# Small products of preparation and readout, one behind each visit of the chain

## The reference

```
zd = z + mu[d] * (shift_seq(z, offset) - z)
r, k, v, lw, la = split(zd)
decay = exp(-exp(-softplus(-(w0[d] + tanh(lw) @ w2[d])) - 0.5))
a = sigmoid(a0[d] + la @ a2[d])
kk = k * k_k;  kk = kk * rsqrt(max(sum_per_head(kk * kk), 1e-24))
k = k * (1 + (a - 1) * k_a)
S = S * decay + (S @ -kk) (kk * a)^T + v k^T;  y = S r     # per token, both directions
bonus = sum_per_head(r * k * r_k) * v
y = (y - mean(y)) * rsqrt(var(y) + eps) * lnx_g + lnx_b + bonus;  y = y * (sigmoid(lg) @ g2)
```

## Time and profile before

| | us |
|---|---|
| median of 3 runs | 3356.26 |
| lowest, highest | 3355.75, 3357.25 |
| profiled execution, its span | 3357.8 |

### The profile page before, as it was taken

How to read it: one execution, slowest core, us unless ns; L and a number is a source line. 1 busy time by engine, 2 the same in 40 slices (tenths; PEclk the granted TensorE clock), 3 DMA queues, 4 the chain that set the end, 5 groups by cost and what they waited for, 6 DMA issues and landing times.

```text
span 3357.8 us, 79208 instructions
## 1 busy us (share of the span) xinstructions
PE 3114.1 (93%) x34382; PEld 2493.0 (74%) x34382; DVE 1500.2 (45%) x2358; ACT 1162.7 (35%) x2403; POOL 831.6 (25%) x518
## 2 busy tenths in 40 slices
PE   7999898999999998999999888989899989989998
PEld 5777676778777786888888666767667667768886
DVE  4455473745444653100144464756565456330033
ACT  4433333423334424211112353434333345342222
POOL 2211111111123132222223221111111243434453
PEclk9999999999999999999999989999999999999999
DMA  5424242434454441111111233413233343522222
GB/s 212 135 97 145 81 142 101 130 121 144 145 166 151 158 169 57 51 63 62 62 50 63 75 101 98 127 63 120 65 122 106 93 140 115 188 69 95 99 88 75
DMA packets 246714, 364.56 MB, mean 109 GB/s; under 512 B 154080, under 2 KB 155376, under 8 KB 245904
## 3 DMA queue, kind: packets, MB, share of 16 engines
q1 hardware_dynamic: 226976, 294.57, 27.6%
q10 hardware_dynamic: 14976, 35.66, 2.7%
q0 software_dynamic: 4464, 29.92, 2.5%
HBM read 290.88 MB, written 69.21 MB: 107 GB/s over the span
## 4 chain that ended last, share of the span: by engine, by line
PE 76%; DVE 6%; issue 5%; ACT 4%; DMA 2%; DVEq 2%; POOLq 2%; PEld 1%; SPq 1%; POOL 0%; PEldq 0%; ACTq 0%
PE banks L281 20%; PE banks L282 18%; PE banks L283 18%; PE banks L1684 2%; PE banks L1023 2%; PE banks L1695 1%; PE banks L1648 1%; PE banks L395 1%; PE banks L1687 1%; PE banks L1745 1%; POOLq L2430 1%; DVE arena L597 1%; PE banks L2057 1%; PE banks L1051 1%; DMA arena<-chunk_inputs 1%
## 5 line engine op out<-in xcount | busy, mean ns | idle before, releaser
L283 PE MATMUL banks<-hx_rounded,slot_rounded 128*128 128x512 f32 (+1 forms) x1624 | 575.1, 354 | 0.0
L906 POOL TENSOR_TENSOR slot_rounded<-slot,branch_weights_high 128x512 fp32r<-128x512 f32 x188 | 251.4, 1357 | 1286.2 <-ACT branch_weights_high L901 1284.9
L281 PE MATMUL banks<-hx_high,weight_parts 128*128 128x512 f32 (+1 forms) x1512 | 537.9, 356 | 10.9 <-DVE hx_low L545 10.4
L281 PE MATMUL banks<-hx_rounded,branch_weights_high 128*128 128x512 f32 (+1 forms) x1280 | 498.8, 390 | 48.1 <-DVE arena L1364 8.6
L282 PE MATMUL banks<-hx_low,weight_parts 128*128 128x512 f32 (+1 forms) x1512 | 538.0, 356 | 0.0
L283 PE MATMUL banks<-hx_high,weight_parts 128*128 128x512 f32 (+1 forms) x1512 | 535.9, 354 | 0.0
L282 PE MATMUL banks<-resid_rounded,branch_weights_high 128*128 128x512 f32 (+1 forms) x1280 | 452.7, 354 | 0.0
L283 PEld LDWEIGHTS banks<-hx_rounded,slot_rounded 128*128 128x128 f32 x1624 | 312.2, 192 | 44.3
L281 PEld LDWEIGHTS banks<-hx_rounded,branch_weights_high 128*128 128x128 f32 x1280 | 245.9, 192 | 128.2 <-issue 75.6
L281 PEld LDWEIGHTS banks<-hx_high,weight_parts 128*128 128x128 f32 x1512 | 286.6, 190 | 55.1 <-issue 14.3
L283 PEld LDWEIGHTS banks<-hx_high,weight_parts 128*128 128x128 f32 x1512 | 286.3, 189 | 41.1
(11 more groups left out here) (263 smaller groups left out, 5853.7 us busy)
## 6 DMA issues: line engine op xcount, KB each, us to landing
slot<-in_w_mix SPq DMA_DIRECT2D x120, 512.0 KB, 3.9
slot<-in_w_ffn_in SPq DMA_DIRECT2D x88, 512.0 KB, 3.3
arena<-chunk_inputs SPq DMA_DIRECT2D x48, 640.0 KB, 4.5
arena<-in_w_ada SPq DMA_DIRECT2D x50, 512.0 KB, 5.1
slot<-in_w_ffn_out SPq DMA_DIRECT2D x44, 512.0 KB, 3.3
slot<-in_w_ada SPq DMA_DIRECT2D x40, 512.0 KB, 4.3
chunk_inputs<-arena SPq DMA_DIRECT2D x80, 256.0 KB, 3.9
arena<-side_projections POOLq DMA_DIRECT2D x16, 1152.0 KB, 6.1
```

Source lines behind the costliest of these rows:

```text
L281: first = nc.tensor.matmul(out, w_hi, x_hi, start=start, stop=False)
L283: return first, nc.tensor.matmul(out, w_lo, x_hi, start=False, stop=stop)
L906: last = nc.gpsimd.tensor_tensor(slots_r[g % 3][:, half], slots[g % 3][:, half], weights_high(g)[:, half], ALU.subtract)
```

## The change

Tiles and small products become two generators. `tiles()` feeds the filler; `smalls()` is asked once behind each visit (or gap), ahead of the fill, and gives one small product, unless the segment being filled has just ended (`left` is 0). The product goes to the bank that is not being filled, whichever segment it is. All tiles go segment 0 first; ScalarE rounds the next weights when segment 0 of a tile has ended (segment 1 where there is no other). The consumers read the bank that was recorded, each at its own product's visit. ScalarE's threads for preparation and readout come ahead of eviction.

```diff
         def tile_order(g):
-            return [0, 1] if (st, t) in ((BODY, 8), (TAIL, 5)) else [1, 0]
+            return [0, 1]
...
             def small(name, s, lhs, rhs, done, taken_by, count=1):
-                at_bank.free(s)
-                nc.tensor.matmul(pair(6)[s], lhs, rhs, start=True, stop=True).then_inc(done.sem, count)
-                at_bank.busy[s] = taken_by
+                b = 1 - at_bank.filling
+                at_bank.free(b)
+                place = place_of[l, st, hp, name, s] = bank[6 + b][:, 0:SEGS[s][1] - SEGS[s][0]]
+                nc.tensor.matmul(place, lhs, rhs, start=True, stop=True).then_inc(done.sem, count)
+                at_bank.busy[b] = taken_by
+                mark((name, s))
+                last_small[0] = where[0]
+                filler.spent += COST[s] * 1.25
...
+            def smalls():
...
                 elif st == BODY:
                     yield from decay_and_rate(0)
-                    yield from tile(0, 1)
+                    yield from reach_gap(last_small[0] + 2)
                     yield from key_norm(0)
-                    yield from tile(0, 0)
-                    yield from tile(1, 1)
-                    yield from tile(1, 0)
+                    yield from reach_gap(last_small[0] + 5)
                     yield from bonus_sum(0)
-                    yield from tile(2, 1)
+                    yield from reach_gap(last_small[0] + 2)
                     yield from decay_and_rate(1)
-                    yield from tile(2, 0)
-                    yield from tile(3, 1)
+                    yield from reach_gap(last_small[0] + 2)
                     yield from key_norm(1)
-                    yield from tile(3, 0)
-                    yield from tile(4, 1)
+                    yield from reach_gap(last_small[0] + 3)
                     yield from bonus_sum(1)
-                    yield from tile(4, 0)
-                    yield from tile(5)
+                    yield from reach_gap(last_small[0] + 4)
...
+            def one_small():
+                if at_bank.left:
+                    next(smalls_left, None)
...
             for v in range(VISITS[st]):
                 chain.visit()
                 where[0] = FREE[st] + v
+                one_small()
                 filler.upto(free + busy * sum(shares[:v + 1]) / sum(shares))
...
             def rounding():
                 for g in range(g0 + 2, g0 + nt + 2):
-                    yield at((g - 2, 1))
+                    yield at((g - 2, 0 if 0 in tile_segs(l, g - 2) else 1))
                     tile_round(act, l, g)
...
-            threads = [Thread(eviction())] + ([Thread(preparation())] if st != TAIL else []) + ([Thread(readout())] if st != PRO else []) + [Thread(rounding())]
+            threads = ([Thread(preparation())] if st != TAIL else []) + ([Thread(readout())] if st != PRO else []) + [Thread(eviction()), Thread(rounding())]
```

More of the change, by code:

```diff
@@ L1057, in key_norm @@
-            def key_norm(d):
-                for i, s in enumerate(sum_order(l, st)):
+                for n, (s, x) in enumerate(((1, 0), (1, 1), (0, 0), (0, 1))):
+                    r = slice(64 * x, 64 * x + 64)
+                    small(("both", d, x), s, SMALL[r, d * P:(d + 1) * P], LD[r, d, SEGS[s][0]:SEGS[s][1]], pre_prod, (pre_act.sem, pre_act.ready(l, hq, 8 * d + n + 1)))
+                    if n == 3 and d == 1 and st == PRO:
+                        nc.tensor.drain().then_inc(small_free.sem, 1)
+                    yield
@@ L1086, in steps, with reach @@
                     at_bank.slot_before = 0
-                    yield from tile(1)
+                    first = 1
+                for t in range(first, TILES_IN[st]):
+                    if (st, t) == (TAIL, 5):
+                        while where[0] < VISITS[TAIL]:
+                            yield None
+                    for s in range(2):
+                        at_tile[0] = (t, s)
+                        yield from tile(t, s)
+            def reach(t, s):
+                while at_tile[0] < (t, s) and not last_call[0]:
+                    yield
@@ L1088, in steps, with reach_gap @@
+            def reach_gap(gap):
+                while where[0] < gap and not last_call[0]:
+                    yield
+            def smalls():
+                if st == PRO:
+                    yield from reach(2, 0)
                     yield from decay_and_rate(0)
-                    yield from tile(2)
+                    yield from reach(3, 0)
                     yield from key_norm(0)
-                    yield from tile(3)
+                    yield from reach(4, 0)
                     yield from bonus_sum(0)
-                    yield from tile(4)
+                    yield from reach(4, 1)
@@ L1094, in steps @@
                     yield from decay_and_rate(1)
-                    nc.tensor.drain().then_inc(small_free.sem, 1)
-                    yield from tile(5)
+                    yield from reach(5, 1)
                     yield from key_norm(1)
-                    yield from tile(6)
+                    yield from reach(6, 1)
                     yield from bonus_sum(1)
-                    for t in range(7, 11):
-                        yield from tile(t)
                 elif st == BODY:
                     yield from decay_and_rate(0)
-                    yield from tile(0, 1)
+                    yield from reach_gap(last_small[0] + 2)
@@ L1114, in steps @@
                     yield from key_norm(1)
[L1115 to L1116 removed]
+                    yield from reach_gap(last_small[0] + 3)
                     yield from bonus_sum(1)
[L1118 to L1119 removed]
+                    yield from reach_gap(last_small[0] + 4)
+                if st != PRO:
+                    if st == TAIL:
+                        yield from reach(4, 1)
                     yield from gate_of_readout()
[L1121 removed]
@@ L1122, in steps @@
-                    yield from tile(7)
-                    while where[0] <= LAST_OF_HEAD:
-                        yield None
+                    yield from reach_gap(LAST_OF_HEAD + 1 if st == BODY else VISITS[TAIL])
                     yield from sum_of_readout(0)
[L1126 to L1129, removed]
+                    yield from reach_gap(last_small[0] + 2)
                     yield from sum_of_readout(1)
[L1131 to L1142, removed]
+            smalls_left = smalls()
```

103 lines of the change are left out of this document (54 added, 49 removed).

## The result

The changed kernel takes 3456.5 us (median of 4 runs, 3452.3 to 3460.7), the kernel before 3356.8 us beside it (3355.8 to 3357.7). The ratio is 1.0286, 95% interval 1.0265 to 1.0307: 96 us slower by the ratio, where 25 were forecast and the range ended 74 above. Lines have moved: the products of `decay_and_rate` and all other small products now stand at L1023, ScalarE's eviction of a segment at L1210, the sigmoid at L1230, the transposes at L1664, the stage load at L1523, the store at L1513, the rounding at L903.

What follows compares the result with a forecast made beforehand. TensorE was taken as the bound, idle mostly at small products. Layer 0 summed to +43 and layer 1 to -18, together +25 on 3356: 3381 us, range 3300 to 3430.

Steps and rivals of the forecast that it cites:

- What went: Layer 0 BODYs lose 35.6 us of small-product waits and most clock loss, -51; layer 1 BODYs -35 and -10.
- First late load: Block 4's load behind store(4, 0) comes late, transposes wait: +22 in layer 0 BODYs, +12 in layer 1.
- Second late load: Block 6's load for the next head pair loses its slack: +12 in layer 0 BODYs, +4 in layer 1.
- Weights behind the late store: Layer 0 BODYs: next_tile(2) behind store(0, 1) comes late, holding ScalarE's rounding and then TensorE at norm 1: +25.
- the clock: BODYs: new waits over 2.5 us cost 2.5 us of clock each, +22 and +10; -15 and -10 regained.
- take the same time: The small products are as many as before and take the same time, so they add nothing.
- PRO there: ... -5: PRO of layer 0: half of the 8.7 us idle goes and little of the clock comes back, -5.
- PRO -10: PRO of layer 1: -10 of 17.2 us idle and 8.5 us of clock.
- None late: Rival: loads and weights have unseen slack or VectorE reaches its steps sooner, 3274 us; chance 0.16.
- VectorE's saturation: Rival: VectorE's lag carries over, some 0.5 us per layer 1 visit up to 26, 3426 us; chance 0.12.
- The table load: Estimate from the skill: late chain 1.4 us longer in three layer 0 stages, 4 us more; left out of the sum.

Runs made afterwards that it cites:

- four measures: Changed kernel with late rounding, block 4's load first, tile 5's weights first, and decay_and_rate(1) of the PROs one segment later: 3356.1 us, ratio 0.9994.
- The run with three edits: Changed kernel with rounding behind a tile's second segment, block 4's load ahead of the stores, and tile 5's weights ahead of store(0, 1): 3364.8 us, ratio 1.0010.
- PRO repairs alone: Changed kernel with, in PRO only, late rounding, decay_and_rate(1) one segment later, and its products spaced in layer 1: 3437.5 us, ratio 1.0225.
- the last run: Four measures plus spaced decay_and_rate products in layer 1's PRO, and key_norm(1) one visit earlier in layer 1's BODYs: 3348.4 us, ratio 0.9963.

## Why the prediction was wrong

**What went.** The wait of `decay_and_rate`'s second half went as forecast. What is left of small waits in the layer 0 BODYs: 86.1 us idle, less the six long waits (53.8) and the short rest of the load row inside the stretch (31.0 - 25.8 - 2.9 = 2.3), less 6.4 that were idle before for other causes (42.0 - 35.6), is 23.6 us; forecast 18. The stage's end is the 2.0 of L1747's row, forecast 2.5. More of it than expected is the ada rows product behind a small product of its bank (5.6, 2.2 and, beside the long ones, 4.2 us). The forecast put a wait between 0.4 and 1.5 us and called 14.4/6 its upper side, but that is 2.4.

**First late load.** Right: 9.1, 8.4 and 8.3 us, 25.8 in all, for 22; the transposes start 5.7 us behind L1446, for 5.9. That the load alone carries it is shown by moving it. In layer 1 the waits are 5.8, 2.9 and 5.4 us, less the 1.3 of before 12.8, for 12.

**Second late load.** Over-sized in layer 0, under-sized in layer 1. In layer 0 it is 0.5, 1.1 and 0.8 us, 2.4 for 12. The long waits ahead of it do not hide it: with four measures, which take them away, it is 1.55 and 1.29 us in the first two BODYs. So the move of two visits did not reach this load in full; where it was absorbed was not tried. In layer 1 it is a failed step that the sum hides: block 6 waits 5.9, 4.1 and 6.5 us, less the 2.2 of before 14.3, for 4. The forecast moved only the first BODY, by VectorE's marks; in the other two the queue stands at `next_tile(4)`, as read above.

**Weights behind the late store.** Right in place, cause and size: 9.4, 9.3 and 9.3 us, 28 for 25. The wait meets L395 of the same bank, not `norm 1`. Moving the load takes it away, and rounding later takes it away too.

So the idle time of the layer 0 BODYs was forecast at -35.6 + 18 + 22 + 12 + 25 = +41, measured +44; that of layer 1 at -35 + 11 + 12 + 4 = -8, measured -9 (52.6 to 43.6). The second agreement is luck: the loads took 27 us more for 16, and all other idle time fell by 36 us for 24.

**The first failed step: the clock.** The sum had -15 and +22 in the layer 0 BODYs, -10 and +10 in layer 1, so 7 in all. The same instructions take 21.0 us and 9.0 us longer, 30 in all: 23 us missed. Not all of it is the clock. In the layer 0 BODYs TensorE works 58.7 us at the lower level, for 30.7 before, in layer 1 40.0 for 23.6; half of the differences is 14 + 8 = 22 us of clock, for 7. The other 8 are not. They are the small products' own time, which the sum put at nothing ("take the same time"): issued one by one they take longer. The run with three edits shows it best, since its clock is higher (0.99) than that of the kernel before (0.97). The 132 small products of the layer 0 BODYs, before at L1023 and at L1051, then at L1023 in that run (length, TensorE's products, their weight loads, PEclk, DMA share, GB/s):

```profile
203.00:763.00 560.00, 34.03 (x84) 14.00 (x84) 0.97 0.37 117
203.00:763.00 560.00, 16.73 (x48) 6.03 (x48) 0.97 0.37 117
215.00:773.00 558.00, 60.88 (x132) 20.25 (x132) 0.99 0.38 119
```

60.9 us for 50.8, in spite of the better clock. The trace does not say why one takes longer alone.

The clock term failed in its rule. "A wait of over 2.5 us cost up to 3.4 us of clock" was read off waits of 2 to 3 us. Behind the load's wait of 8.4 us, in windows:

```profile
498.00:505.00 7.00, 0.40 (x2) 0.40 (x3) 0.89 (x1) 0.00 (x0) 0.00 (x0) 0.51 0.71 217
505.00:510.00 5.00, 4.16 (x22) 2.23 (x24) 0.00 (x0) 2.62 (x9) 0.00 (x0) 0.50 0.03 11
510.00:515.00 5.00, 5.00 (x76) 4.11 (x72) 0.71 (x2) 1.34 (x5) 0.00 (x0) 0.50 0.34 108
515.00:525.00 10.00, 10.00 (x165) 7.61 (x159) 8.47 (x14) 1.55 (x3) 0.00 (x0) 0.99 0.10 41
```

The clock stays at its lower level (1.2 GHz) for 10 us after TensorE works again, which costs 5. Taking that wait away gave 12.5 us in this BODY for a wait of 8.4, and 16.6 in the first (20.8 less the 4.2 ahead of it) for one of 9.1.

**The second failed step, and the larger: the PROs.** "PRO there: ... -5" and "PRO -10" became +20 and +15: 50 us of the 76 missed. (The clock and the products' own time are 23, idle time in the BODYs some 2.) I counted the marks of BODY and took the PROs for a plain gain, though two such things move there as well: when the weights are rounded, and what the store must have read before a sigmoid writes its tile. The repairs in PRO give 20 us by ratio; in that run's trace 12 us (layer 0) and 8 us (layer 1) over the kernel before stay. A part of them is the clock and nothing else. The PRO of layer 0 is the same code in the run with PRO repairs alone and in that with four measures:

```profile
82.00:214.00 132.00, 118.91 (x1112) 92.33 (x1110) 56.49 (x79) 44.49 (x84) 26.54 (x21) 0.93 0.38 115
```
```profile
82.00:207.40 125.40, 113.09 (x1110) 88.14 (x1108) 56.51 (x79) 44.36 (x84) 26.37 (x20) 0.99 0.40 121
```

5.8 of the 6.6 us between them are TensorE's own busy time. What sets the one clock or the other was not settled. In the change's PRO, behind the wait of 3.21 us:

```profile
88.00:93.00 5.00, 4.40 (x7) 1.47 (x7) 0.00 (x0) 1.25 (x2) 0.50 (x1) 0.56 0.00 0
93.00:98.00 5.00, 4.82 (x14) 3.30 (x15) 2.98 (x4) 1.43 (x4) 0.00 (x0) 0.50 0.00 0
98.00:103.00 5.00, 5.00 (x20) 4.34 (x19) 1.68 (x2) 4.70 (x7) 1.57 (x2) 0.58 0.00 0
```

0.44 + 0.50 + 0.42, times 5, is 6.8 us for a wait of 3.2, where the earlier trace rows gave 3.4.

**The rivals.** "None late" was to give 3274; the run with four measures comes to 3356 and the best to 3348. By stretches, in us, each ending with the start of a transposes block:

| | before | change | four measures |
|---|---|---|---|
| PRO of layer 0, from 82 | 120.3 | 140.6 | 125.4 |
| BODYs of layer 0 | 561.6 | 626.3 | 553.9 |
| last block of layer 0 to the first BODY of layer 1 | 1240.2 | 1255.3 | 1252.5 |
| BODYs of layer 1 | 484.0 | 486.3 | 465.2 |

The run with four measures is not quite "none late": block 6 of the layer 1 BODYs still waits 5.4, 3.7 and 6.0 us, and these 15 us are the difference between the 34 us forecast there and the 19 gained. In layer 0 the gain is small, for 33 forecast: the same BODY code took 554, 558, 557, 560 and 565 us in five traces. In the 554 us, idle time is 37.4 us for 42.0 (the short waits come back at other places), and of the 12 us that the clock gives back the products' own time takes 9. The two PROs, forecast at -15, still cost 17 us. VectorE's saturation did not decide it: the runs that take a wait away get all of it, TensorE's waits for VectorE in the change's layer 1 BODYs sum to 2.6 us, and where the last run moved a mark one visit earlier VectorE's last step ended 4.1 us earlier. The measured time lies beyond even its 3426, for other reasons.

**The table load.** The row at 536.12 takes 1.28 us and the Square starts 0.01 us behind its end, as in the earlier trace rows. The Trainium skill (ScalarE: Activation LUTs, "What ACT_TABLE_LOAD costs") adds a drain of about 1.38 us to each switch; this trace, too, has none between the table load and the next activation.

## What to carry to other kernels

When an edit shifts marks, list every queue whose order is fixed against them (loads, stores, the engine that rounds what was loaded), in every stage, the first and smallest too: here one reordered load was worth 56 us. An in-place buffer that a store still reads sets an earliest time; moved a visit too early, it costs as much as moved too late. A long wait of TensorE costs more than its length: the clock behind it took 1.5 us more for the 9.3 us wait at L395, 5 us more for the 8.4 us one and 6.8 us more for one of 3.2 us. And a small product that is moved may itself take longer: 132 of them took 10 us more when each was issued alone.

## What the runs showed of the hardware

The price of the lower clock level is not a fixed one per wait. In the kernel before, in the layer 1 BODYs, TensorE was at 1.2 GHz for 3.4 us behind each of six waits of 1.4 to 2.5 us. In the change it was there for 10 us after the end of the 8.4 us wait at block 4, and for 13.7 us behind a wait of 3.2 us in the PRO, where the products that followed were spread and waited again (0.78 us at 93.18). Around the wait of 9.3 us at L395, with denser tile products behind it, it was there for 10.2 us in all, 7.2 of them during the wait.

Nor is it the same in each execution. Behind the wait of block 2 in the first BODY of layer 0 (2.9 us in both) there were 10.2 us at 1.2 GHz in the change and none in the run with the load of block 4 first, where code and wait up to there are the same: 35.7 us for 31.5 to the next block. So a difference of some 5 us between two traces is not by itself the work of an edit.
